# Turning rows and activations on VectorE, and dealing the expert weights to two DMA queues

## The reference

```python
def expert_block(args):                 # for each block of rows of one expert
    xb, e = args
    h = (xb @ w_up[e] + b_up[e]).reshape(MOE_BLOCK, D_FF, 2)
    x_glu = jnp.minimum(h[..., 0], SWIGLU_LIMIT)
    x_lin = jnp.clip(h[..., 1], -SWIGLU_LIMIT, SWIGLU_LIMIT)
    act = x_glu * jax.nn.sigmoid(SWIGLU_ALPHA * x_glu) * (x_lin + 1)
    return act @ w_down[e] + b_down[e]
```

## Time and profile before

| | |
|---|---|
| time, median of 3 runs | 1594.34 us |
| time of the profiled execution | 1594.16 us |
| its span | 1592.1 us (2.1 us lie around it) |
| TensorE busy | 1545.8 us (97%) |
| VectorE busy | 361.1 us (23%) |
| ScalarE busy | 294.3 us (18%) |
| GpSimd busy | 92.8 us (6%) |
| moved by DMA | 474.09 MB, mean 298 GB/s |
| hardware queue used | q1, 455.68 MB (SP's) |

### The profile page before, as it was taken

How to read it: one execution, slowest core, us unless ns; L and a number is a source line. 1 busy time by engine, 2 the same in 40 slices (tenths; PEclk the granted TensorE clock), 3 DMA queues, 4 the chain that set the end, 5 groups by cost and what they waited for, 6 DMA issues and landing times.

```text
span 1592.1 us, 38358 instructions
## 1 busy us (share of the span) xinstructions
PE 1545.8 (97%) x16674; PEld 887.8 (56%) x16674; DVE 361.1 (23%) x716; ACT 294.3 (18%) x538; POOL 92.8 (6%) x130
## 2 busy tenths in 40 slices
PE   6999999979999999999999999999999999999988
PEld 5999999978544343444343444343444343443487
DVE  5357333343411100011000111000101000111264
ACT  5333322321111001011010101010101010110155
POOL 0000000000000100000100000000101000101000
PEclk9999999989999999999999999999999999999999
DMA  8311222342989999999999999999999999999441
GB/s 267 137 54 54 81 80 92 124 172 94 341 343 391 395 386 395 391 386 384 392 388 394 391 379 387 389 388 392 388 378 389 383 393 389 389 380 395 158 158 44
DMA packets 80504, 474.09 MB, mean 298 GB/s; under 512 B 13806, under 2 KB 18518, under 8 KB 27348
## 3 DMA queue, kind: packets, MB, share of 16 engines
q1 hardware_dynamic: 73188, 455.68, 73.3%
q0 software_dynamic: 7168, 17.56, 4.8%
q10 hardware_dynamic: 96, 0.07, 0.0%
HBM read 461.02 MB, written 20.88 MB: 303 GB/s over the span
## 4 chain that ended last, share of the span: by engine, by line
PE 91%; DVE 3%; DMA 2%; ACT 2%; issue 1%; SPq 1%; POOLq 0%; DVEq 0%; ACTq 0%
PE ps L2161 42%; PE ps L2171 20%; PE ps L1799 10%; PE ps L1988 3%; PE ps L1749 2%; PE ps L1750 2%; PE ps L1751 2%; PE ps L2158 2%; PE ps L2141 2%; PE ps L2149 2%; DMA raw<-w_ple_chunks 1%; PE ps L1862 1%; ACT S L788 1%; DMA xg<-m_rows,iug 1%; DVE S L1186 1%
## 5 line engine op out<-in xcount | busy, mean ns | idle before, releaser
L2161 PE MATMUL ps<-raw,xT 128*32 128x512 f32 x6144 | 672.2, 593 | 0.0
L2161 PEld LDWEIGHTS ps<-raw,xT 128*32 128x32 f32 x6144 | 193.2, 110 | 438.8 <-issue 438.8
L2171 PE MATMUL ps<-raw,acT 128*32 128x256 f32 x6144 | 338.4, 380 | 1.3 <-ACT acT L973 1.3
L2171 PEld LDWEIGHTS ps<-raw,acT 128*32 128x32 f32 x6144 | 196.3, 110 | 131.3 <-ACT acT L973 1.6
L1574 DVE TENSOR_SCALAR gl<-ps 128x256 f32<-128x256 f32 x96 | 34.8, 418 | 738.0 <-ACT gl L967 738.0
L1799 PE MATMUL ps<-aTh,wh 128*128 128x272 f32 x512 | 108.4, 293 | 0.0
L1799 PE MATMUL ps<-aTh,wl 128*128 128x272 f32 x512 | 106.9, 290 | 0.0
L1799 PE MATMUL ps<-aTl,wh 128*128 128x272 f32 x512 | 106.6, 290 | 0.0
L1587 DVE TENSOR_SCALAR yrow<-ps,gside 32x256 f32<-32x256 f32 x93 | 45.6, 490 | 220.3 <-PE ps L2171 219.4
L973 ACT ACTIVATE acT<-ps 128x512 f32<-128x512 f32 x64 | 27.9, 488 | 347.4 <-PE ps L2149 347.4
L960 ACT ACTIVATE xT<-ps 128x768 f32<-128x768 f32 x33 | 26.8, 811 | 348.7 <-PE ps L2141 348.7
(11 more groups left out here) (371 smaller groups left out, 1347.8 us busy)
## 6 DMA issues: line engine op xcount, KB each, us to landing
raw<-w_up SPq DMA_DIRECT2D x256, 1024.0 KB, 10.1
raw<-w_down_rows SPq DMA_DIRECT2D x128, 1024.0 KB, 10.6
raw<-w_mix SPq DMA_DIRECT2D x25, 1024.0 KB, 4.8
raw<-w_ple_chunks SPq DMA_DIRECT2D x4, 1024.0 KB, 10.2
xin<-x_prompt SPq DMA_DIRECT2D x4, 512.0 KB, 6.3
hrow<-x_prompt SPq DMA_DIRECT2D x1, 2048.0 KB, 7.8
h_rows<-hrow SPq DMA_DIRECT2D x4, 512.0 KB, 2.6
m_rows<-mrow SPq DMA_DIRECT2D x4, 512.0 KB, 2.6
```

What stands on the lines that cost most here:

```text
L2161: ins = mmul(ps[32 * j:32 * j + 32, b, :], xT[:, k, 32 * g:32 * g + 32], raw[k][:, 512 * q:512 * q + 512], start=False, stop=(k == UPC - 1))
L2171: ins = mmul(ps[32 * j:32 * j + 32, 3 + b, 0:LB], a, raw[slot][:, D * (k % 2) + LB * q:D * (k % 2) + LB * q + LB], start=(k == 0), stop=(k ...
```

## The change

- `tx` and `ta` leave TensorE, `xh_copy` and `ah_copy` leave ScalarE. In their place VectorE has `turn_x` (12 transposes of 32 x 32 squares, each instruction 32 partitions x 256 elements) and `turn_act` (16 instructions, each 32 partitions x 192 elements), from SBUF to SBUF.
- The places of these: `turn_act(i-1)` ahead of `linear(i)`, `turn_x(i+1)` between `linear(i)` and `swiglu(i)`. Behind the loop `turn_act(nb-1)` writes a tile of its own, `acT2`, behind `gsum`. Ahead of the loop `turn_x(0)` stands before `slot_entries`, `turn_x(1)` before `linear(0)`.
- GpSimd's gathers and SP's load of `bd3` wait on `xh_done` in place of `tx_done`. TensorE waits on `ah_done` once ahead of the down chunks.
- SP issues the weight chunks with even numbers only (`range(0, ..., 2)`). ScalarE's program issues the odd ones: `odd_up(i+1)` behind `y_copy`, `odd_down(i)` behind `silu(i)`. They go to ScalarE's own hardware queue. The chunks of block 0 and the last four down chunks stay with SP. ScalarE runs its last `body` outside the loop, with no issues, and reads its expert numbers from `tabE` in the loop.

```diff
+            def odd_up(e, used_up):
+                for l in range(1, UPC, 2):
+                    act.wait_ge(tiles_done, used_up + l + 1)
+                    act.dma_start(raw[l][:], w_up[bass.ds(e, 1), l].rearrange("e p n -> (e p) n")).then_inc(landed[l], 16)
+            def odd_down(e, used_down):
+                for c in range(1, DNC, 2):
+                    act.wait_ge(tiles_done, used_down + c + 1)
+                    act.dma_start(raw[UPC + c][:], w_dn[bass.ds(e, 1), c].rearrange("e p n -> (e p) n")).then_inc(landed[UPC + c], 16)
@@ ScalarE, body(i)
                     y_copy(i - 2, TB + 12 * i - 4)
-                ah_copy(i - 1)
-                xh_copy(i + 1, TB + 12 * i + 4)
+                if not last:
+                    odd_up(expert_of(i + 1), TB + 12 * i - 4)
                 silu(i, TB + 12 * i + 4)
+                if not last:
+                    odd_down(expert_of(i), TB + 12 * i + 4)
@@ VectorE
+            def turn_x(b, up_done):
+                dve.wait_ge(gathered, 16 * b + 16)
+                if up_done is not None:
+                    dve.wait_ge(tiles_done, up_done)
+                for g in range(SETS):
+                    for r in range(4):
+                        ins = nc.vector.transpose(xT[32 * r:32 * r + 32, :, 32 * g:32 * g + 32],
+                                                  xg[32 * g:32 * g + 32, :].rearrange("p (k n) -> p k n", n=P)[:, :, 32 * r:32 * r + 32])
+                ins.then_inc(xh_done, 1)
+            def turn_act(dst, i):
+                dve.wait_ge(act_rows, SETS * i + SETS)
+                for g in range(4):
+                    for r in range(4):
+                        ins = nc.vector.transpose(dst[32 * r:32 * r + 32, :, 32 * g:32 * g + 32],
+                                                  arow[32 * g:32 * g + 32, :].rearrange("p (k n) -> p k n", n=P)[:, :, 32 * r:32 * r + 32])
+                ins.then_inc(ah_done, 1)
@@ VectorE, body(i)
                     side_rows(i - 2, TB + 12 * i - 4)
+                turn_act(acT, i - 1)
                 linear(i)
+                turn_x(i + 1, TB + 12 * i + 4)
                 swiglu(i)
@@ TensorE, body(i)
                     up_chunk(l)
-                    if l == 3:
-                        ta(i - 1)
-                    if l == UPC - 1:
-                        pe.wait_ge(ah_done, 2 * i)
-                        tx(i + 1)
+                pe.wait_ge(ah_done, i)
@@ SP, body(i)
-                for l in range(UPC if first else BLK):
+                for l in range(0, UPC if first else BLK, 2):
```

More of the change, by code:

```diff
@@ L193, in build @@
         acT = at("acT", [P, 2 * SETS, P], F32, R0 + 4096)
+        acT2 = at("acT2", [P, 2 * SETS, P], F32, R0 + 8192)
         yrow = at("yrow", [P, D], F32, R0 + 12288)
@@ L399, in build @@
         gathered = sem("gathered")
-        tx_done = sem("tx_done")
         xh_done = sem("xh_done")
@@ L404, in build @@
         act_rows = sem("act_rows")
-        ta_done = sem("ta_done")
         ah_done = sem("ah_done")
@@ L603, in _ @@
                 sp.dma_start(raw[l][:], w_dn[bass.ds(e_prev, 1), l].rearrange("e p n -> (e p) n")).then_inc(landed[l], 16)
-            sp.wait_ge(tx_done, nb + 1)
+            sp.wait_ge(xh_done, nb + 1)
             for g in range(3):
@@ L678, in _ @@
             pool.wait_ge(row1_step, 2)
-            pool.wait_ge(tx_done, 1)
+            pool.wait_ge(xh_done, 1)
             rows_from(ius[0:CAP, 0:1])
@@ L685, in _ @@
             for b in range(2, PEEL + 1):
-                pool.wait_ge(tx_done, b)
+                pool.wait_ge(xh_done, b)
                 rows_from(rowi[0:CAP, b:b + 1])
@@ L692, in _ @@
             with pool.Fori(PEEL, end) as i:
-                pool.wait_ge(tx_done, i + 1)
+                pool.wait_ge(xh_done, i + 1)
                 gather(i + 1)
@@ L952, in _ @@
             nc.scalar.activation(ev[:], ev[:], ACT.Exp).then_inc(r_exp, 1)
[L955 to L960, removed]
             def silu(i, up_done):
@@ L967, in silu @@
                     nc.scalar.activation(gl[:, 0, b, :], src, ACT.Silu, scale=ALPHA).then_inc(silu_done, 1)
[L969 to L974, removed]
             def y_copy(b, chunk_done):
@@ L986, in _ @@
             pp_copy(3)
-            xh_copy(0, None)
             pp_copy(4)
@@ L990, in _, with expert_of, body @@
             act.wait_ge(rows_out[0], 96)
-            xh_copy(1, TB + 8)
+            w_up = A["w_up"][0].rearrange("e (k p) n -> e k p n", p=P)
+            w_dn = A["w_down_rows"]
+            def expert_of(i):
+                if isinstance(i, int):
+                    return i
+                return act.value_load(tabE[0:1, bass.ds(i, 1)], min_val=0, max_val=NEXP - 1)
+            def odd_up(e, used_up):
[6 more added lines that the diff above has]
+                    act.dma_start(raw[UPC + c][:], w_dn[bass.ds(e, 1), c].rearrange("e p n -> (e p) n")).then_inc(landed[UPC + c], 16)
+            odd_up(1, TB)
             silu(0, TB + 8)
-            def body(i, first):
+            def body(i, first, last):
                 if not first:
@@ L998, in body @@
                     y_copy(i - 2, TB + 12 * i - 4)
-                ah_copy(i - 1)
-                xh_copy(i + 1, TB + 12 * i + 4)
+                if not last:
+                    odd_up(expert_of(i + 1), TB + 12 * i - 4)
                 silu(i, TB + 12 * i + 4)
-            body(1, True)
-            body(2, False)
-            end = act.value_load(tabN[0:1, 0:1], min_val=NEXP, max_val=NEXP + MAXOVER)
+                if not last:
+                    odd_down(expert_of(i), TB + 12 * i + 4)
+            body(1, True, False)
+            body(2, False, False)
+            act.wait_ge(tab_done, 1)
+            stop = act.value_load(tabN[0:1, 2:3], min_val=NEXP - 1, max_val=NEXP + MAXOVER - 1)
             nb = act.value_load(tabN[0:1, 1:2], min_val=NEXP - PEEL, max_val=NEXP + MAXOVER - PEEL) + PEEL
-            with act.Fori(PEEL, end) as i:
-                body(i, False)
+            with act.Fori(PEEL, stop) as i:
+                body(i, False, False)
+            body(nb - 1, False, True)
             def round_ple(g):
@@ L1026, in _ @@
             nc.scalar.activation(gate3[CAP:P], gside[CAP:P, :, bass.ds(nb - 1, 1)].rearrange("p s b -> p (s b)"), ACT.Copy).then_inc(pick_in, 1)
-            ah_copy(nb - 1)
+            act.wait_ge(pick_in, 1)
             act.wait_ge(gs_tr, 1)
@@ L1524, in _ @@
             nc.vector.tensor_scalar(tabN[:, 0:1], ps[0:1, 3, 64:65], float(NEXP), None, ALU.add)
+            nc.vector.tensor_scalar(tabN[:, 2:3], ps[0:1, 3, 64:65], float(NEXP - 1), None, ALU.add)
             nc.vector.tensor_scalar(tabN[:, 1:2], ps[0:1, 3, 64:65], float(NEXP - PEEL), None, ALU.add).then_inc(tab_done, 1)
@@ L1589, in side_rows @@
                 ins.then_inc(y_side, 1)
+            def turn_x(b, up_done):
[14 more added lines that the diff above has]
+                ins.then_inc(ah_done, 1)
             second_rows()
+            turn_x(0, None)
             slot_entries()
             slot_hots(range(0, NT))
+            turn_x(1, TB + 8)
             linear(0)
@@ L1621, in split_ple @@
                   .then_inc(split_done, 1)
+            turn_act(acT2, nb - 1)
             dve.wait_ge(gs_hi, 1)
@@ L2135, in _ @@
             project_ple(3, (0,))
[L2138 to L2150, removed]
             def groups(b):
@@ L2163, in up_chunk, with down_chunk @@
                 ins.then_inc(tiles_done, 1)
-            def down_chunk(c, slot):
+            def down_chunk(acT, c, slot):
                 for k in (2 * c, 2 * c + 1):
@@ L2196, in _ @@
             project_ple(3, (1,))
-            tx(0)
             project_ple(4)
@@ L2208, in _ @@
                 up_chunk(k)
-                if k == UPC - 1:
-                    tx(1)
             pe.wait_ge(pp_ev, NT)
@@ L2234, in body @@
                     pe.wait_ge(landed[UPC + c], 16 * i)
-                    down_chunk(c, UPC + c)
+                    down_chunk(acT, c, UPC + c)
             body(1, True)
@@ L2245, in _ @@
             pe.wait_ge(xh_done, nb + 1)
-            ta(nb - 1)
+            pe.wait_ge(ah_done, nb)
             pe.wait_ge(y_done, nb - 1)
@@ L2250, in _ @@
                 pe.wait_ge(landed[c], 16 * used[c] + 16 * nb + 16)
-                if c % 2 == 0:
-                    pe.wait_ge(ah_done, 2 * nb - 1 + c // 2)
-                down_chunk(c, c)
+                down_chunk(acT2, c, c)
                 if c == 1:
```

## The result

| | before | after |
|---|---|---|
| time, median (range) | 1594.08 us (1592.27 to 1595.96, 10 runs) | 1598.16 us (1595.72 to 1600.65, 10 runs) |
| profiled execution, span | 1594.16, 1592.1 us | 1595.80, 1593.8 us |
| TensorE / VectorE / ScalarE busy | 97% / 23% / 18% | 94% / 45% / 15% |

After against before is 1.0026, with a 95% interval of 1.0016 to 1.0035: 0.26% slower, where 0.7% faster was forecast. The time lies inside the stated range (1553 to 1604); it is the direction that was wrong. The profiled execution is one of the quicker ones of its kernel, so its trace shows 1.6 us of the loss and the medians show 4.1.

A forecast was written before the change was run, and what follows sets the result against it. TensorE was taken as the bound, with the saturated weight stream equal at about 33.9 us a block. A gain of 17.6 us in the loop less 6.6 in the tail gave 11.0 off 1594.16: 1583.2 us, range 1553 to 1604.

The forecast's parts named there:

- the lead: Last up chunk of block 31 lands at 1466.7, TensorE takes it up at 1485.8; these 19.1 us can be won.
- U: End of the up chunks of block 31, 1488.4 before; forecast to move 17.6 us, to near 1471.
- The other term: Weight stream split over two queues: rate forecast unchanged, within bounds of 314 to 423+ GB/s.
- What bounds the kernel: In the loop, TensorE and saturated DMA engines both need about 33.9 us a block, equal by chance.
- Turns on VectorE: `turn_x` 5.0 us (4.4 to 6.0), `turn_act` 5.8 us (4.3 to 6.4), hidden in the loop.
- The start: Block 0 slowed about 1.7 us by the clock, block 1 2.4 us late at 451.3; 1.5 us counted.
- The tail: Behind the loop, VectorE's added turns start `side_rows` of block 30 6.6 us later (bounds 4.5 and 8.2).
- R1: Rival: the stream can follow, TensorE stays the bound, 40.4 us less, 1553.8; 0.25 together with times between it and the forecast.
- R2: Rival: two queues cost rate in the stream from about 460 to 1485, slower than before; chance 0.20.
- price list: Each 1% of stream rate costs 10.2 us once the lead is gone; decides from 1.1%; 3% gives 1613.8.
- R3: Rival: no gain, as turns take twice as long or the stream loses 1%: 1593 to 1594; 0.10 with neighbours.

The follow-up runs named there:

- The experiment with the extra loads moved: After, with SP's `bup` of every block and the 1 MB `gate_r[0]` load issued by ScalarE instead: 1600.01 us, 1.0046 of before.
- the evenly loaded kernel: After, with the 1 MB `gate_r[0]` load and `bup` each issued half by SP, half by ScalarE: 1593.6 us, 1.0001 of before.

## Why the prediction was wrong

**The step that failed** is the lead in "U moves by 19.1 - 1.5 = 17.6 us": the premise, under "If the DMA engines hold their rate, U can't be earlier than the lead allows: 19.1 us", that these 19.1 us can be used whole. U moved by 4.5 us. In one queue, which serves chunks in the order in which TensorE needs them, the lead can be used: U moved by 16.95 us, to 1471.45. In two queues it can't. The other term, "The bounds are therefore 314 to 423+ GB/s, and I take the value of the stream now, no change", held against before (388 GB/s for 386 to 387 in 850 to 1420), but not against the same kernel with one queue (391 to 392). The second queue was taken as a question of rate alone; that it is also one of order was not among the rivals.

**The mechanism.** While both queues have work they get about equal shares, whatever is needed first. In the DMA view of after, 500 to 680, the last numbers are packets, MB and share of the engines:

```profile
q10 hardware_dynamic: 4756, 34.65, 47.6%
q1 hardware_dynamic: 4762, 34.14, 47.2%
```

The packets are equal, though q1's chunks had fallen behind by then (26.5 us to landing for 17.5). The totals over 485 to 1400, 171.08 MB on q1 and 170.21 on q10, don't show it, since TensorE takes from the two in turn and so both move the same number of chunks per block. But SP's queue also has the 1 MB and `bup`. As TensorE gains on the stream, requests pile up where the surplus is: SP's six places are all waiting (30.6 us of a block of 33.9), and odd chunks land 30.6 - 16.5 = 14 us sooner than even ones. At 33.8 / 6 = 5.6 us for a place these are 2.5 chunks of the lead of 12 places that lie in SBUF, landed and of no use yet. The experiment with the extra loads moved flips the queues, the one with shared loads removes most of the gap and 4.6 us. Why the gap grows from 4.5 to 14 us is shown in part only: at equal packets q1 moved 0.51 MB less in 500 to 680, some 2.7 us at its 190 GB/s (an estimate).

**The sum of it**, an estimate. Measured from the start of block 1, block 31 starts at 1010.9 us in after and at 996.3 with one queue, 14.6 later. Of this 2.5 chunks of 1.05 MB at 392 GB/s are 6.7 us, and 359.36 - 356.51 = 2.85 MB that were moved less are 7.3 us; together 14.0. For the evenly loaded kernel the same working gives 1.6 + 6.6 = 8.2 against 9.4 measured. The two parts split one difference by bookkeeping, and the split is rough: 13.0 of the 14.6 us are lost by block 13 (400.85 us from block 1 against 387.86), and only 1.6 behind it, though the traffic stays lower. That less is moved in two queues than in one, with the turns on VectorE, is shown by the stretches; what causes it is not settled.

**Point by point.**

- What bounds the kernel: right. TensorE and a saturated stream, equal by chance, a lead of 19.1 us, gone after about 12 blocks. With one queue: block 12, U at 1471.45 for a forecast of about 1471, 1583.16 us for 1583.2.
- Turns on VectorE: `turn_x` 5.37 us for 5.0, `turn_act` 6.11 for 5.8, inside the bounds, and fully hidden in the loop (910.00 `linear`, 911.12 `turn_x`, needed at about 919).
- The Trainium skill's rule (VectorE: DVE Perf Modes, section "Two Vector instructions with no wait between them") puts the turns at the upper side. The trace agrees in direction: 12 of them take 5.37 us, 0.45 each, for a mean of 435 ns of one, so nothing overlaps; but the upper bound, 0.50, is not reached, as a turn itself is cheaper than the row it was taken from.
- The start: block 1 at 451.36 for 451.3. TensorE's granted clock was 0.50 in 420 to 424, the lower level, after 6.35 us idle, and block 0's up chunks took 22.23 us for 20.81, 1.4 us for 1.7 forecast.
- The tail: `side_rows` at U + 18.9 for 18.2, 7.3 us later for 6.6. One wait was not seen. The last down chunks were forecast at U + 15.7 and started at U + 20.6, since their PSUM is freed by `side_rows` (10.22 us idle). They then ran their first group in 6.67 us for 5.39, at a granted clock of 0.50 in 1497 to 1506.
- R1 (the stream can follow) is out with two queues and with one. R2 had the right sign and the right place, and its price list holds for a part: 0.8% of rate is 8 us by its 10.2 us for 1%. But by that price rate alone would have left the result at 1591, faster than before; it took the lost order too. R3 is out: the turns cost what they should.
- The Trainium skill (DMA: Bandwidth & Descriptors, section "Issuing engines are not separate DMA queues") would have made the split worth nothing. The run with two queues and the transposes on TensorE agrees (1.0001); after against one queue, 15.0 us, does not. The Trainium skill (DMA: Bandwidth & Descriptors, section "Queues, rings and completion order") says that a DMA engine goes round between its queues packet by packet. The trace agrees: 4762 and 4756 packets in 500 to 680.

## What to carry to other kernels

When loads are requested far ahead and the DMA engines are saturated, keep them in one queue in the order of use: here a second queue added no rate, and whichever queue had more in it held back every other chunk. Before a lead is counted as a gain, ask in which order it is served. Work that is moved to an idle engine is free in the loop and has to be priced in the tail, where the last round can often be left out.

## What was not expected of the hardware

- With the turns on VectorE, two saturated hardware queues move 0.7 to 0.8% less than one (388 against 391 to 392 GB/s). With the transposes on TensorE both kernels, one queue and two, move 386 to 387.
- An imbalance of one 1 MB load in 340 MB (and of 16 KB a block for `bup`) is not worked off: the gap between the queues grew from 4.5 us at 485 to 14 at 900, and it was 15.0 in 1300 to 1340.
- A transpose on VectorE in fp32, 32 partitions, takes 435 ns for 256 elements and 370 for 192, by these two sizes about 1.0 ns per element over a fixed part of some 175 ns (an estimate).
